# A hybrid encoder layer on one core: another order of work inside three of its four layer norms

## The chip, the cores and the metric

The kernel runs on one core of one Trainium2 chip. The metric is the device time of one execution in microseconds (us); of several executions the median is taken. A core has five engines that run at the same time and meet only through semaphores: PE (TensorE, matrix products; PEld are its weight loads), DVE (VectorE), ACT (ScalarE), POOL (GpSimd) and SP (SyncE, which here only starts transfers). An engine takes its own instructions strictly in the order in which they are written, so a waiting instruction holds up all that is written behind it.

## What is computed

512 tokens and 16 meta tokens of width 1024 go through one layer with three residual parts and four layer norms:

```python
h = layer_norm(concat([meta, x]), ln_in)                       # norm 0
h = layer_norm(A*h + 0.5*swiglu(h, gate1, up1, down1), ffn1)   # norm 1
h = layer_norm(A*h + token_mixer(h), mix)                      # norm 2
h = layer_norm(A*h + 0.5*swiglu(h, gate2, up2, down2), ffn2)   # norm 3
return h[:, N_META:]

def layer_norm(x, g, b):
    mu = mean(x)
    xc = x - mu
    return xc * rsqrt(mean(xc*xc) + eps) * g + b
```

The hidden width of a SwiGLU is 2816. The token mixer projects h, runs windowed attention and a gated linear attention in two directions, and projects back with w_out. A is the fourth root of 2. All of it is float32 in the reference.

## The kernel before

Everything is kept transposed: 128 of the 1024 features on the partitions, tokens along the free dimension, so h (`H`), the sum before a norm (`X`) and its scaled copies (`xs`) are 8 tiles of 128x528 (128x512 from norm 2 on, where the meta tokens are dropped). A product in float32 precision is made of three float16 products: weights and activations are each scaled by a power of two and split into a high part (f16) and a low part (the rest).

**Weights.** They come in 73 chunks into two slots of `stage`, in float32. For each chunk `c` DVE takes the largest magnitude of a partition (`chunk_max`, L1308, cmax), POOL takes it over all partitions (L1842, call), DVE makes the scale out of it in four small steps and the factor that undoes it in a fifth (`chunk_scale`: L1290 to L1295 and L1336), ACT writes the high part (`split_hi`, L951), and DVE the low part (`chunk_lo`, L1330), whose semaphore `w_ready` lets PE use the chunk and SP load the next chunk into its slot. The last tiles of each residual product are therefore followed by the weight work for the next stage: by norm 1 chunks IN0 and IN0+1 of w_in, by norm 2 chunks GU[1] and GU[1]+1 of the second SwiGLU.

**A layer norm** (norm L, tokens in two halves h = 0, 1). DVE adds each finished residual tile to a running sum; the last tile (7) is written in halves (`residual_tile`, L1359). PE gets the mean over the partitions by products with a constant matrix (L455, L465). DVE subtracts the mean in 8 steps for each half (`centre`, L1257). ACT squares these 8 tiles (L918), PE sums the squares (L470, 8 float32 products, recorded as 16), ACT takes the root of a half (L932, std), DVE its reciprocal (L1277, rstd). ACT's order is: squares of half 0, root of half 0, squares of half 1, root of half 1. Only when both reciprocals are there does DVE multiply tile by tile (L1281), ACT write `xs` (L943) and `H` (L945), and DVE the low part of `xs` (L1271); the first products of the next stage follow tile by tile. After four tiles ACT puts in the high part of the next weight chunk, for which it needs that chunk's scale.

**Tables.** ACT has one set of function tables loaded at a time. Before an activation whose function is not in it, the compiler puts an ACT_TABLE_LOAD. The root and the SiLU of the SwiGLU are in different sets.

The order of every engine's work is written out by hand; no scheduler is at work.

## Time and profile before

| | |
|---|---|
| median of 3 runs | 1099.26 us |
| the three runs | 1098.03, 1099.26, 1104.86 us |
| the profiled execution | 1098.44 us |
| its span, first to last instruction | 1096.6 us |
| mean granted clock of TensorE, of full speed | 0.972 |
| PE busy | 1005.5 us, 92% |
| DVE busy | 730.0 us, 67% |
| ACT busy | 385.6 us, 35% |
| table loads of ACT | 15, each 1283 ns |

The profiled execution lies 1.84 us above its own span (start and end of the program) and 0.82 us below the median of the three runs. PE is busy for nearly all of the span; the four layer norms are where it stands still, since nothing of the next stage can start before the norm is done.

### The profile page before, as it was taken

The numbers are of one execution on the slowest core, as the hardware profiler recorded it, in microseconds if no ns is written. First come the engines' busy times: TensorE is split into PE (matmuls) and PEld (weight loads), VectorE is DVE, ScalarE is ACT, GpSimd is POOL, SyncE is SP. The second block draws the span as 40 slices with busy tenths as digits, with TensorE's granted clock in tenths as the row PEclk, the third lists the DMA queues.
The fourth block names the chain that finished last, engine by engine and source line by source line (L and its number), as shares of the span: only waits on it lengthen the run. The fifth ranks groups of instructions, "written<-read, shape, count | busy, mean of one in ns | idle before, by whom it ended". The sixth has DMA issues, their size and how long they took to land.

```text
span 1096.6 us, 16402 instructions
## 1 busy us (share of the span) xinstructions
PE 1005.5 (92%) x6604; PEld 658.2 (60%) x6604; DVE 730.0 (67%) x1188; ACT 385.6 (35%) x492; POOL 33.8 (3%) x96
## 2 busy tenths in 40 slices
PE   2799999999899997999996889779999999989995
PEld 1588888888688874895565434434444444434443
DVE  7756666668865657777658857676666666876645
ACT  2722222224511117655234742362222222541105
POOL 1000000000000000000000000000000000000000
PEclk9899999999899998999998989889999999999998
DMA  4232232323313220221211002213232232312202
GB/s 157 71 114 101 90 111 80 115 77 140 109 54 106 96 77 1 78 78 40 76 40 39 1 1 77 77 39 113 79 115 103 88 115 90 145 56 103 105 1 78
DMA packets 25168, 88.70 MB, mean 81 GB/s; under 512 B 2859, under 2 KB 5123, under 8 KB 25123
## 3 DMA queue, kind: packets, MB, share of 16 engines
q1 hardware_dynamic: 24256, 87.24, 22.7%
q10 hardware_dynamic: 867, 0.85, 0.3%
q8 instruction: 29, 0.48, 0.2%
q14 instruction: 16, 0.13, 0.0%
HBM read 85.99 MB, written 2.10 MB: 80 GB/s over the span
## 4 chain that ended last, share of the span: by engine, by line
PE 75%; DVE 15%; ACT 7%; issue 2%; DMA 1%; ACTq 0%; POOL 0%; DVEq 0%
PE PS L485 35%; PE PS L521 20%; PE PS L576 8%; PE PS L872 3%; DVE cmax L1308 3%; DVE wsp L1330 3%; PE PS L470 2%; ACT wsp L951 2%; ACT H L945 2%; DVE X L1257 1%; PE PS L560 1%; PE PS L850 1%; DVE big L1408 1%; ACT xs L943 1%; PE PS L698 1%
## 5 line engine op out<-in xcount | busy, mean ns | idle before, releaser
L485 PE MATMUL PS<-xs,wsp 128*128 128x264 f16 (+1 forms) x3168 | 471.6, 312 | 12.8 <-ACT xs L943 8.1
L485 PEld LDWEIGHTS PS<-xs,wsp 128*128 128x128 f16 x3168 | 310.6, 98 | 173.8 <-issue 13.5
L951 ACT ACTIVATE wsp<-stage,wscale 128x2048 f16<-128x2048 f32 (+2 forms) x73 | 156.5, 2144 | 370.5 <-DVE wscale L1294 198.6
L1330 DVE SCALAR_TENSOR_TENSOR wsp<-stage,wscale,wsp 128x2048 f16<-128x2048 f32 (+2 forms) x73 | 184.6, 2529 | 113.9 <-ACT wsp L951 113.9
L521 PE MATMUL PS<-big,wsp 128*128 128x264 f16 (+1 forms) x1584 | 238.5, 314 | 11.6 <-DVE big L1408 9.5
L521 PEld LDWEIGHTS PS<-big,wsp 128*128 128x128 f16 x1584 | 155.8, 99 | 94.0 <-DVE big L1408 12.8
L1308 DVE TENSOR_REDUCE cmax<-stage 128x1 f32<-128x2048 f32 (+2 forms) x73 | 179.7, 2461 | 3.9
L1342 DVE SCALAR_TENSOR_TENSOR big<-PS,oscale,tmp_a 128x528 f32 (+3 forms) x44 | 33.4, 758 | 75.8 <-ACT tmp_a L958 75.8
L958 ACT ACTIVATE tmp_a<-PS,oscale 128x528 f32<-128x528 f32 (+1 forms) x44 | 30.5, 693 | 135.9 <-PE PS L485 135.9
L576 PE MATMUL PS<-xs,wsp 128*128 128x264 f16 (+1 forms) x384 | 67.0, 328 | 0.1
L1842 POOL PARTITION_ALL_REDUCE call<-cmax x73 | 29.5, 404 | 984.2 <-DVE cmax L1308 984.2
L470 PE MATMUL PS<-tmp_b,ones 128*128 128x264 f32 (+1 forms) x128 | 36.2, 445 | 17.5 <-ACT tmp_b L918 17.5
L576 PEld LDWEIGHTS PS<-xs,wsp 128*128 128x128 f16 x384 | 35.8, 98 | 24.4 <-issue 1.9
L872 PE MATMUL PS<-xs,wsp 128*128 128x512 f16 x192 | 42.4, 379 | 3.2 <-DVE X L1354 2.1
L470 PEld LDWEIGHTS PS<-tmp_b,ones 128*128 128x128 f32 x128 | 27.9, 223 | 26.1 <-ACT tmp_b L918 21.1
L918 ACT ACTIVATE tmp_b<-X 128x264 f32<-128x264 f32 (+1 forms) x64 | 23.9, 416 | 49.5 <-DVE X L1257 45.7
L576 PE MATMUL PS<-wsp,xs 128*88 128x256 f16 (+2 forms) x408 | 39.5, 257 | 1.7 <-ACT kT L1013 1.7
L981 ACT ACTIVATE big<-big,hscale 128x528 f16<-128x528 f32 (+1 forms) x44 | 30.3, 722 | 29.1 <-DVE big L1408 26.5
L576 PEld LDWEIGHTS PS<-wsp,xs 128*88 128x88 f16 (+2 forms) x408 | 38.0, 113 | 3.5 <-ACT kT L1013 2.5
L1408 DVE SCALAR_TENSOR_TENSOR big<-big,hscale 128x528 f16<-128x528 f32 (+1 forms) x44 | 31.6, 755 | 5.0 <-ACT big L981 3.8
L872 PEld LDWEIGHTS PS<-xs,wsp 128*128 128x128 f16 x192 | 18.5, 98 | 26.8 <-DVE wsp L1330 2.6
L1366 DVE SCALAR_TENSOR_TENSOR X<-PS,oscale,H 128x528 f32<-128x528 f32 (+1 forms) x16 | 12.2, 760 | 27.5 <-PE PS L521 27.4
(178 smaller groups left out, 694.4 us busy)
## 6 DMA issues: line engine op xcount, KB each, us to landing
stage<-in_gate SPq DMA_DIRECT2D x44, 512.0 KB, 3.7
stage<-in_up SPq DMA_DIRECT2D x44, 512.0 KB, 4.5
stage<-in_down SPq DMA_DIRECT2D x32, 704.0 KB, 4.9
stage<-in_w_in SPq DMA_DIRECT2D x16, 512.0 KB, 4.6
stage<-in_w_out SPq DMA_DIRECT2D x8, 512.0 KB, 4.3
X<-in_xT SPq DMA_DIRECT2D x2, 1056.0 KB, 6.9
out_T<-H SPq DMA_DIRECT2D x8, 256.0 KB, 2.0
stage<-in_w_in SPq DMA_DIRECT2D x2, 576.0 KB, 4.3
```

The lines of the kernel that those rows point to most:

```text
L470: nc.tensor.matmul(PS[:, ln_bank(L, 1, h), 0:ln_width(L)], ones[:, :], squares[:, n % 4, 0:ln_width(L)], start=k == 0, stop=k == KD - 1).t ...
L485: return nc.tensor.matmul(dst, w, x, start=k == 0 and wp + xp == 0, stop=k == KD - 1 and xp == 1)
L521: mm = nc.tensor.matmul(dst, w(wp, k), x, start=k in (0, split_at) and wp + xp == 0, stop=k + 1 in (kt, split_at) and xp == 1)
L576: mm = nc.tensor.matmul(dst, x if lhs_is_x else w, w if lhs_is_x else x, start=k == 0 and wp + xp == 0, stop=k == KD - 1 and xp == 1)
L872: mm = nc.tensor.matmul(acc(1, 2 * (n % 2)), w, tokens(1, xs[:, xp, k, :]), start=gla and k == REP and wp + xp == 0, stop=not gla and k == ...
L951: nc.scalar.activation(wsp[:, slot, 0, 0:cols], stage[:, slot, 0:cols], ACT.Copy, scale=wscale[:, slot:slot + 1]).then_inc(w_hi, 1)
L958: nc.scalar.activation(tokens(f, tmp_a[:, s, :]), acc(f, 4 * s), ACT.Silu, scale=oscale[:, slot:slot + 1]).then_inc(silu_ready, 1)
L981: nc.scalar.activation(hid_s[:, m, 0, ln_cols(2 * f)], hid[:, m + 2, ln_cols(2 * f)], ACT.Copy, scale=hscale[:, i:i + 1]).then_inc(hs_hi, 1)
L1308: nc.vector.tensor_reduce(cmax[:, one], stage[:, slot, 0:cols], AX.X, ALU.max, apply_absolute_value=True).then_inc(w_max, 1)
L1330: nc.vector.scalar_tensor_tensor(wsp[:, slot, 1, 0:cols], stage[:, slot, 0:cols], wscale[:, one], wsp[:, slot, 0, 0:cols], ALU.mult, ALU.s ...
L1342: nc.vector.scalar_tensor_tensor(tokens(f, hid[:, m + 2, :]), acc(f, 4 * s + 2), oscale[:, slot:slot + 1], tokens(f, tmp_a[:, s, :]), ALU. ...
L1408: nc.vector.scalar_tensor_tensor(hid_s[:, m, 1, t], hid[:, m + 2, t], hscale[:, i:i + 1], hid_s[:, m, 0, t], ALU.mult, ALU.subtract).then_ ...
```

## The change

Four edits:

- In norm 1 and norm 2 DVE's `chunk_max` of the second weight chunk moves from ahead of the centring to behind it.
- In the same norms `chunk_scale` of that chunk moves from ahead of the two reciprocals to behind them.
- In the last pass of the out projection, `chunk_lo` of chunk GU[1] moves from behind residual tile 7 to ahead of it.
- In every norm ACT gets one more instruction, a root of one column of a constant into an unused column of `warm`, ahead of the first square. It waits for nothing in norms 1 to 3.

```diff
@@ sb("warm") @@
-        warm = sb("warm", [P, 2])
+        warm = sb("warm", [P, 5])
@@ scalar: layer_norm(L) @@
                 if L == 0:
                     act.wait_ge(par_loaded, 16)
                     act.wait_ge(ready0, 6)
+                nc.scalar.activation(warm[:, L + 1:L + 2], eps[:, 1:2], ACT.Sqrt).then_inc(warmed, 1)
                 for h in range(2):
@@ vector: layer_norm(L, chunk) @@
                 if L:
                     for h in range(2):
                         centre(L, h)
-                if chunk is not None:
+                if L in (1, 2):
+                    c = (IN0, GU[1])[L - 1] + 1
+                    chunk_max(c, c % 2, c // 2, KD * 2 * P)
+                if chunk is not None and L == 0:
                     chunk_scale(*chunk)
...
                     nc.vector.reciprocal(rstd[:, half], std[:, half]).then_inc(rstd_ready, 1)
+                if chunk is not None and L:
+                    chunk_scale(*chunk)
                 dve.wait_ge(rstd_ready, 2 * L + 2)
@@ vector: main order @@
             ffn(0)
-            chunk_max(IN0 + 1, (IN0 + 1) % 2, (IN0 + 1) // 2, KD * 2 * P)
             layer_norm(1, (IN0 + 1, (IN0 + 1) % 2, XF_INQ))
...
                 for t in range(2):
+                    if last and t:
+                        chunk_lo(c + 1, (c + 1) % 2, cols)
                     residual_tile(2 * n + t, t, KD + 2 * n + t, c % 2, 2)
 
-            chunk_lo(GU[1], GU[1] % 2, GU_COLS)
-            chunk_max(GU[1] + 1, (GU[1] + 1) % 2, (GU[1] + 1) // 2, GU_COLS)
             layer_norm(2, (GU[1] + 1, (GU[1] + 1) % 2, XF_GU[1]))
```

How the rows of the engines move, with each kernel's own line numbers (a line of the changed kernel is up to 6 higher). First DVE from the last residual tile (X<-PS,oscale_b,X) to the multiplication (X<-X,stats) in norm 1; before, then with the change:

```order
L1359 SCALAR_TENSOR_TENSOR X<-PS,oscale_b,X 128x264 x2
L1308 TENSOR_REDUCE cmax<-stage 128x1
L1257 TENSOR_TENSOR X<-X,PS 128x264 x16
L1290 TENSOR_SCALAR cexp<-call 128x1
L1292 TENSOR_SCALAR cneg<-cexp 128x1
L1294 TENSOR_SCALAR wscale<-cneg 128x1
L1295 TENSOR_SCALAR winv<-cneg 128x1
L1336 TENSOR_TENSOR oscale<-winv,xinv 128x1
L1277 RECIPROCAL stats<-stats 128x264 x2
L1281 TENSOR_TENSOR X<-X,stats 128x528 x3
```
```order
L1365 SCALAR_TENSOR_TENSOR X<-PS,oscale_b,X 128x264 x2
L1258 TENSOR_TENSOR X<-X,PS 128x264 x16
L1314 TENSOR_REDUCE cmax<-stage 128x1
L1281 RECIPROCAL stats<-stats 128x264 x2
L1296 TENSOR_SCALAR cexp<-call 128x1
L1298 TENSOR_SCALAR cneg<-cexp 128x1
L1300 TENSOR_SCALAR wscale<-cneg 128x1
L1301 TENSOR_SCALAR winv<-cneg 128x1
L1342 TENSOR_TENSOR oscale<-winv,xinv 128x1
L1287 TENSOR_TENSOR X<-X,stats 128x528 x3
```

The maximum (cmax) has gone behind the 16 steps of centring (X<-X,PS), and the five small steps behind the two reciprocals, directly ahead of the multiplication.

DVE in the same place of norm 2, from the last running sum (stats<-stats,X) to the reciprocals; before, then with the change:

```order
L1250 TENSOR_TENSOR stats<-stats,X 128x512
L1359 SCALAR_TENSOR_TENSOR X<-PS,oscale,H 128x256 x2
L1330 SCALAR_TENSOR_TENSOR wsp<-stage,wscale,wsp 128x2048
L1308 TENSOR_REDUCE cmax<-stage 128x1
L1257 TENSOR_TENSOR X<-X,PS 128x256 x16
L1290 TENSOR_SCALAR cexp<-call 128x1
```
```order
L1251 TENSOR_TENSOR stats<-stats,X 128x512
L1336 SCALAR_TENSOR_TENSOR wsp<-stage,wscale,wsp 128x2048
L1365 SCALAR_TENSOR_TENSOR X<-PS,oscale,H 128x256 x2
L1258 TENSOR_TENSOR X<-X,PS 128x256 x16
L1314 TENSOR_REDUCE cmax<-stage 128x1
L1281 RECIPROCAL stats<-stats 128x256 x2
```

The low part (wsp<-stage,wscale,wsp) now stands ahead of the last residual tile (X<-PS,oscale,H in halves), the maximum behind the centring.

ACT from the last weight chunk of the first SwiGLU's stage to the second root of norm 1; before, then with the change:

```order
L951 ACTIVATE wsp<-stage,wscale 128x2304
L918 ACTIVATE tmp_b<-X 128x264 x8
L932 ACT_TABLE_LOAD
L932 ACTIVATE stats<-PS,eps 128x264
L918 ACTIVATE tmp_b<-X 128x264 x8
L932 ACTIVATE stats<-PS,eps 128x264
```
```order
L952 ACTIVATE wsp<-stage,wscale 128x2304
L925 ACT_TABLE_LOAD
L925 ACTIVATE warm<-eps 128x1
L918 ACTIVATE tmp_b<-X 128x264 x8
L933 ACTIVATE stats<-PS,eps 128x264
L918 ACTIVATE tmp_b<-X 128x264 x8
L933 ACTIVATE stats<-PS,eps 128x264
```

The table load has gone from between squares and root to ahead of the squares, together with the new one-column root. At the start of the kernel (norm 0) two loads stood before, one ahead of the squares and one ahead of the root:

```order
L918 ACT_TABLE_LOAD
L918 ACTIVATE tmp_b<-X 128x264 x8
L951 ACTIVATE wsp<-stage,wscale 128x2048
L932 ACT_TABLE_LOAD
L932 ACTIVATE stats<-PS,eps 128x264
```
```order
L925 ACT_TABLE_LOAD
L925 ACTIVATE warm<-eps 128x1
L918 ACTIVATE tmp_b<-X 128x264 x8
L952 ACTIVATE wsp<-stage,wscale 128x2048
L933 ACTIVATE stats<-PS,eps 128x264
```

Of these two one is left, ahead of the one-column root. In all, ACT_TABLE_LOAD stands 15 times before and 14 times with the change; nothing on PE, POOL or SP has moved.

## Rows read from the trace of the kernel before

**Rows 1.** The page: the chain of work that ended last, shares by engine.

```profile
...
PE 75%; DVE 15%; ACT 7%; issue 2%; DMA 1%; ACTq 0%; POOL 0%; DVEq 0%
...
```

**Rows 2.** Timeline, norm 1: start us, us, engine line op tiles xcount [idle<-releaser].

```profile
...
408.75 0.89 DVE L1359 SCALAR_TENSOR_TENSOR X<-PS,oscale_b,X 128x264 f32<-128x264 f32 x2 [2.12 <-PE PS L521]
...
409.56 2.28 DVE L1308 TENSOR_REDUCE cmax<-stage 128x1 f32<-128x2048 f32 x1
411.75 5.51 DVE L1257 TENSOR_TENSOR X<-X,PS 128x264 f32<-128x264 f32 x16
...
412.20 3.05 ACT L918 ACTIVATE tmp_b<-X 128x264 f32<-128x264 f32 x8 [11.77 <-DVE X L1257]
...
412.68 3.83 PE L470 MATMUL PS<-tmp_b,ones 128*128 128x264 f32 x16 [2.22 <-ACT tmp_b L918]
415.27 1.28 ACT L932 ACT_TABLE_LOAD   x1
416.56 0.48 ACT L932 ACTIVATE stats<-PS,eps 128x264 f32<-128x264 f32 x1
...
417.18 0.14 DVE L1290 TENSOR_SCALAR cexp<-call 128x1 int32<-128x1 int32 x1
...
417.88 1.80 DVE L1277 RECIPROCAL stats<-stats 128x264 f32<-128x264 f32 x1
...
421.79 1.80 DVE L1277 RECIPROCAL stats<-stats 128x264 f32<-128x264 f32 x1 [2.11 <-ACT stats L932]
423.62 1.95 DVE L1281 TENSOR_TENSOR X<-X,stats 128x528 f32<-128x528 f32 x3
...
```

**Rows 3.** Timeline of norm 2, with the residual tiles ahead of it.

```profile
...
690.45 2.00 ACT L951 ACTIVATE wsp<-stage,wscale 128x2048 f16<-128x2048 f32 x1 [8.53 <-DVE winv L1295]
...
696.65 0.88 DVE L1359 SCALAR_TENSOR_TENSOR X<-PS,oscale,H 128x256 f32<-128x256 f32 x2 [4.50 <-PE PS L872]
...
697.45 2.34 DVE L1330 SCALAR_TENSOR_TENSOR wsp<-stage,wscale,wsp 128x2048 f16<-128x2048 f32 x1
...
701.90 5.38 DVE L1257 TENSOR_TENSOR X<-X,PS 128x256 f32<-128x256 f32 x16
...
702.81 6.25 PE L470 MATMUL PS<-tmp_b,ones 128*128 128x256 f32 x16 [4.49 <-ACT tmp_b L918]
...
709.10 0.47 ACT L932 ACTIVATE stats<-PS,eps 128x256 f32<-128x256 f32 x1 [0.69 <-PE PS L470]
...
714.20 1.75 DVE L1277 RECIPROCAL stats<-stats 128x256 f32<-128x256 f32 x1 [2.84 <-ACT stats L932]
...
```

**Rows 4.** Timeline of norm 3, which has no weight work in it.

```profile
...
1074.75 0.88 DVE L1359 SCALAR_TENSOR_TENSOR X<-PS,oscale_b,X 128x256 f32<-128x256 f32 x2 [2.03 <-PE PS L521]
...
1076.02 5.39 DVE L1257 TENSOR_TENSOR X<-X,PS 128x256 f32<-128x256 f32 x16 [0.40 <-PE PS L465]
...
1076.95 3.72 PE L470 MATMUL PS<-tmp_b,ones 128*128 128x256 f32 x16 [0.53 <-ACT tmp_b L918]
...
1080.77 0.47 ACT L932 ACTIVATE stats<-PS,eps 128x256 f32<-128x256 f32 x1
...
```

**Rows 5.** Timeline of norm 0, ACT alone.

```profile
...
16.41 1.28 ACT L918 ACT_TABLE_LOAD   x1 [16.41 <-DVE X L1257]
...
24.06 2.00 ACT L951 ACTIVATE wsp<-stage,wscale 128x2048 f16<-128x2048 f32 x1 [1.49 <-DVE wscale L1294]
26.08 1.28 ACT L932 ACT_TABLE_LOAD   x1
27.38 0.48 ACT L932 ACTIVATE stats<-PS,eps 128x264 f32<-128x264 f32 x1
...
```

**Rows 6.** Windows: from:to us, busy PE, PEld, DVE, ACT, POOL; PEclk, DMA, GB/s.

```profile
...
425.30:431.00 5.70, 5.27 (x22) 2.62 (x23) 5.17 (x9) 5.70 (x8) 0.00 (x0) 0.50 0.00 0
...
698.40:702.80 4.40, 0.00 (x0) 0.00 (x0) 4.40 (x5) 0.46 (x2) 0.35 (x1) 0.81 0.36 120
702.80:709.00 6.20, 6.19 (x16) 4.78 (x16) 5.07 (x19) 3.90 (x8) 0.00 (x0) 0.58 0.23 89
...
```

## The prediction

> **What bounds the kernel now.** I read the page first. Its chain of waits gives three quarters of the span to PE [rows 1], and PE is busy for 92% of it: inside the SwiGLUs and projections the kernel runs at PE's pace, and work taken from DVE or ACT there buys nothing. The change touches only the layer norms, so I went to the timelines of the four norms and asked at each step which of two inputs came last. Since all that follows a norm starts from its output tiles, a norm that ends x us earlier moves the rest of the program by x, unless the clock of PE changes too; so I read the granted clock in windows last.
>
> In norm 1 [rows 2] the reader should see DVE finish the last residual tile, take the weight maximum for 2.28 us, and only then begin to centre, at 411.75. PE has had the means long before: norm 3 has no weight work, and there centring begins 1.27 us after the last residual tile has begun (1074.75 to 1076.02) [rows 4]. The squares follow the first centred tile, PE's sums the first square, and the root the last sum. From the first root to the end ACT and PE set the pace: the second half's squares stand behind the first root in ACT's order, and the second reciprocal waited 2.11 us for its root. Norm 2 [rows 3] has two pieces of weight work ahead of the centring, the low part (2.34 us) and the maximum.
>
> The table load in norm 1 looks as if it were on the path, since the root follows it at once. It isn't alone there: it ends at 416.55, and PE's sums end at 412.68 + 3.83 = 416.51 [rows 2]. Take away either one, and the other still holds the root.
>
> **The change, part by part.** All times are offsets within one profiled execution.
>
> *Norm 0: the table load.* Before, ACT writes a weight chunk's high part from 24.06 to 26.06, loads the table at 26.08 and takes the root at 27.38 [rows 5]. The root shows no idle time before it, so the sums of its half were there, and the high part waited for DVE's scale, which does not move; the load alone is on the path, and without it the root comes 27.38 - 26.08 = 1.30 us earlier. The other load, ahead of the first square at 16.41, also goes ahead of the wait for DVE, into time in which ACT has nothing to do. That makes the first squares 1.28 us earlier and gains nothing more, because ACT then waits for the scale. **1.30 us gained.**
> What the ScalarE page of the Trainium skill ("ScalarE: Activation LUTs", section "What ACT_TABLE_LOAD costs") says speaks for more: a switch costs the 1283 ns load and some 1380 ns of drain, 2.66 us in all. The trace shows no drain here, since the root starts 0.02 us after the load [rows 5]; by the page the gain of norm 0 would be 2.66 and the time 1088.6.
>
> *Norm 1: the maximum behind the centring.* Centring starts at 408.75 + 1.27 = 410.02 in place of 411.75: 1.73 us earlier. Squares and sums follow, PE's from 410.95 to 414.78; the table is already there, so the root comes with the same 0.05 us after the sums, at about 414.82, 1.74 us earlier than 416.56. The second reciprocal moves with it, from 421.79 to 420.05. Is DVE free by then? Centring until 415.53, maximum until about 417.7, first reciprocal until about 419.5: free 0.6 us before it is wanted. So the maximum, 2.28 us that lay on the path, now fits into a wait, with 0.6 us to spare. The load itself goes to where ACT stood still for 11.77 us ahead of the squares [rows 2]. That covers its 1.28 us and the new root of one column, which costs between nothing and the 0.48 us of a root of 264 columns; without that cover both would delay the first square.
>
> *Norm 1: the scale behind the reciprocals.* Here is a cost. The five small steps took 0.70 us, from 417.18 to 417.88 [rows 2], while DVE had nothing urgent to do. Now they stand between the second reciprocal and the first multiplication, where nothing covers them. DVE starts an instruction that waits for nothing about 0.1 us before the last one is over (the maximum starts at 409.56, before 409.64), and the multiplication started 0.03 us after the reciprocal; so of the 0.70 I take 0.60 as added. The bounds are 0.5 (a second overlap) and 0.8 (none, and a wait). The weight maximum is over 4 us old by then, so POOL is no issue; ACT needs the scale only after four tiles. **1.74 - 0.60 = 1.14 us gained.**
>
> *Norm 2: two pieces out of the way.* The low part moves ahead of residual tile 7. It needs ACT's high part, done at 692.45, and DVE stood still for 4.50 us before 696.65, since 692.15 [rows 3]: it runs from about 692.5 to 694.8, 1.8 us before PE delivers tile 7, so the residual tile is not delayed. SP may then load the next chunk 5 us earlier, into a slot that nobody reads any more. Centring starts at 696.65 + 1.27 = 697.92 in place of 701.90: 3.98 us earlier.
>
> *Norm 2: the clock.* PE's sums for the first half took 6.25 us here [rows 3], against 3.72 in norm 3 [rows 4]. The windows say why: after 4.4 us without a product the granted clock began to fall (0.81), and during the sums it was 0.58 of full speed, so 1.2 GHz for most of it [rows 6]. With the change PE stands still for about 0.5 us between means and sums, as in norm 3, where the sums ran at 2.4 GHz. I take 3.72. The sums then run from 698.83 to 702.55 and the root comes at 702.59 instead of 709.10: 6.51 us earlier, 3.98 of it from order and 2.53 from the clock. DVE has the same 0.6 us to spare as in norm 1. Less 0.60 for the scale steps: **5.91 us gained**, the largest term.
>
> *Norm 3.* No weight work, one table load, ending at the same time as the sums (1076.95 + 3.72 = 1080.67, root at 1080.77) [rows 4]: **0.06 us gained.**
>
> **The sum:** 1.30 + 1.14 + 5.91 + 0.06 = 8.41 us. The profiled execution took 1098.44 us: 1090.0. It lies 0.82 under the median of the three runs, so a median of the new kernel may come out some tenths higher.
>
> **Rivals.**
>
> *The clock stays low in norm 2's first sums.* Then they take 6.25 us as now, and the gain falls by 2.53: **1092.6**. For it: the clock is already falling in some norms when the sums come. Against it: norm 1 had a stop of 2.22 us before its sums, longer than the 0.5 us expected here, and still needed only 3.83 us for them [rows 2]. Chance 0.10.
>
> *DVE becomes the bound inside the norm.* If maximum and first reciprocal used up more than the 0.6 us to spare, for instance because the maximum's chunk or DVE's own start comes later by a microsecond, each of the two norms would lose some 0.2 to 1 us, say 1.5 in all: **1091.5**. For it speaks only that the margin is small. Chance 0.06.
>
> *The clock is dealt better.* After norm 1 the first projection products ran at half clock (0.50 from 425.3 to 431) and were PE's to finish [rows 6]; half a stretch of 5.7 us less is 1.4 us of products less, if PE bounds them throughout: **1088.6**. Chance 0.12.
>
> *A table switch costs more than its load.* In norm 0 there is room for little: from the end of the high part to the root it is 1.32 us [rows 5], and the root may overlap the high part by 0.1, which makes 1.42 in place of 1.30: **1089.9**. Chance 0.02. This is what the rows leave of the drain in the page on ScalarE of the Trainium skill.
>
> *Slower than before.* One mechanism could do it: PE's stop between the sums and the next stage grows by the 0.60 us of the scale steps in norms 1 and 2, the clock falls sooner, and the low stretch after it lasts longer, in products that PE bounds. At half clock each us of such a stretch costs 0.5 us. The 8.41 us are used up once low clock in such products has grown by 16.8 us; the one after norm 1 holds at least 5.7 us now [rows 6]. So it would have to more than triple in norm 1, or be dealt anew all over the kernel, where the mean clock of 0.972 means 31 us at 2.4 GHz lost so far, of which a quarter more would have to come. **1099 to 1101**. The shown runs of the same program (1098.03, 1098.44 profiled, 1099.26) speak against so large a redeal, one at 1104.86 leaves room. "TensorE: Matmul & The Clock Gate" of the Trainium skill (section "What's actually happening") goes further than these runs: one kernel meets a different number of slow products from run to run, which would argue for a larger chance; the runs shown don't bear it out beyond 1.2 us, the last one apart. Chance 0.03; a milder form, 3 to 6 us lost (**1093 to 1096**), gets 0.06.
>
> *The change doesn't do what it says* would mean that a second load appears ahead of the squares, because square and root are in different sets. The instruction order rules it out: one load in each norm, none between squares and root.
>
> **How the numbers follow.** My forecast, all terms as summed, has 0.61 and by itself spans 1089 to 1091. Faster than that are the better clock and, barely, the dearer switch (0.14), slower the rest (0.25). For 8 in 10 the range goes down to 1087.6, which takes in the better clock and bounds of the small terms, and up to 1094.0, past the low clock in norm 2 and the DVE rival; the rest of the slower cases is outside. A measurement of this kernel tells a difference of about 1%, 11 us, from none. The forecast is 0.8%, so within: 0.90. Faster by over 1% would be under 1088.3, which needs the better clock in both places: 0.08. Slower by over 1%: 0.02.
>
> **What the new profile would show.** Norm 0: no load between high part and root, root near 26.1. Norm 1: centring 1.3 us after the last residual tile, maximum behind it, root right at the end of the sums, and the five small steps with about 0.6 us between second reciprocal and multiplication. Norm 2: low part ended before tile 7's residual starts, sums in 3.7 us at full clock. From the start of the last residual tile to the first multiplication it should take 13.7 us in norm 1 in place of 14.87 (408.75 to 423.62), and to the second reciprocal 11.0 us in norm 2 in place of 17.55 (696.65 to 714.20). Wrong would be: sums of 6 us in norm 2, a reciprocal that starts late behind the maximum, or norms that are shorter as said while the end does not move, which would put the loss into PE's clock in the stages between.

## The result and the profile after

The changed kernel took 1095.09 us, the median of 20 runs (1089.35 to 1096.02); the kernel before took 1098.52 in the same sessions, the median of 20 (1095.64 to 1104.86). The ratio is 0.9948, with a 95% interval of 0.9931 to 0.9965: a gain of 0.5%. That is 5.7 us by the means (1093.5 against 1099.2) and 3.4 us by the medians, where 8.4 were forecast. The median lies 1.1 us above the stated range; carried over by the ratio to the 1099.26 us known at the time of the forecast, the time is 1093.5 us, 0.5 inside it.

The single times say more than the median. They fall into two groups with nothing between: 7 of 20 at 1089.35 to 1090.80, with a mean granted clock of 0.969 to 0.973, and 13 of 20 at 1094.83 to 1096.02, with 0.966 to 0.968. The forecast of 1090.0 is the time of the lower group (mean 1090.0). The profiled execution is of the upper one: 1095.9 us, span 1094.1, clock 0.966, against 1098.44, 1096.6 and 0.972 before.

Inside the norms the profile after shows what was forecast. The timeline of norm 1, columns as in [rows 2]:

```profile
...
407.35 0.89 DVE L1365 SCALAR_TENSOR_TENSOR X<-PS,oscale_b,X 128x264 f32<-128x264 f32 x2 [2.12 <-PE PS L521]
...
408.64 5.53 DVE L1258 TENSOR_TENSOR X<-X,PS 128x264 f32<-128x264 f32 x16 [0.41 <-PE PS L465]
...
409.58 3.83 PE L470 MATMUL PS<-tmp_b,ones 128*128 128x264 f32 x16 [0.53 <-ACT tmp_b L918]
413.45 0.48 ACT L933 ACTIVATE stats<-PS,eps 128x264 f32<-128x264 f32 x1 [1.29 <-PE PS L470]
...
414.08 2.28 DVE L1314 TENSOR_REDUCE cmax<-stage 128x1 f32<-128x2048 f32 x1
...
416.27 1.80 DVE L1281 RECIPROCAL stats<-stats 128x264 f32<-128x264 f32 x1
...
418.67 1.80 DVE L1281 RECIPROCAL stats<-stats 128x264 f32<-128x264 f32 x1 [0.60 <-ACT stats L933]
420.39 0.10 DVE L1296 TENSOR_SCALAR cexp<-call 128x1 int32<-128x1 int32 x1
...
421.05 1.95 DVE L1287 TENSOR_TENSOR X<-X,stats 128x528 f32<-128x528 f32 x3
...
```

Centring begins 1.29 us after the last residual tile (408.64 - 407.35), where [rows 2] had 3.00; PE's stop before the sums is 0.53 in place of 2.22; the root comes right behind the sums, the maximum runs behind the centring and the first reciprocal behind it. The second reciprocal waited 0.60 us, so DVE had the margin that was forecast. Between its start and the multiplication lie 2.38 us, against 1.83 before: 0.55 for the five scale steps. From residual tile to multiplication: 13.70 us, 14.87 before.

The timeline of norm 2, which answers to [rows 3]:

```profile
...
695.36 2.35 DVE L1336 SCALAR_TENSOR_TENSOR wsp<-stage,wscale,wsp 128x2048 f16<-128x2048 f32 x1 [0.32 <-ACT wsp L952]
...
699.54 0.88 DVE L1365 SCALAR_TENSOR_TENSOR X<-PS,oscale,H 128x256 f32<-128x256 f32 x2 [1.82 <-PE PS L872]
...
700.81 5.39 DVE L1258 TENSOR_TENSOR X<-X,PS 128x256 f32<-128x256 f32 x16 [0.40 <-PE PS L465]
...
701.74 3.72 PE L470 MATMUL PS<-tmp_b,ones 128*128 128x256 f32 x16 [0.53 <-ACT tmp_b L918]
705.50 0.47 ACT L933 ACTIVATE stats<-PS,eps 128x256 f32<-128x256 f32 x1 [1.25 <-PE PS L470]
...
710.59 1.75 DVE L1281 RECIPROCAL stats<-stats 128x256 f32<-128x256 f32 x1 [0.53 <-ACT stats L933]
...
712.92 1.90 DVE L1287 TENSOR_TENSOR X<-X,stats 128x512 f32<-128x512 f32 x3
...
```

The low part ended at 697.71, 1.83 us before the residual tile. The sums took 3.72 us in place of 6.25 and the second reciprocal began 11.05 us after the residual tile. To the multiplication: 13.38 us, 19.33 before.

The timelines of norm 3 and, below it, of ACT alone in norm 0 answer to [rows 4] and [rows 5]:

```profile
...
1072.34 0.88 DVE L1365 SCALAR_TENSOR_TENSOR X<-PS,oscale_b,X 128x256 f32<-128x256 f32 x2 [2.03 <-PE PS L521]
...
1078.30 0.47 ACT L933 ACTIVATE stats<-PS,eps 128x256 f32<-128x256 f32 x1 [1.25 <-PE PS L470]
...
```

ACT in norm 0:

```profile
...
23.94 2.00 ACT L952 ACTIVATE wsp<-stage,wscale 128x2048 f16<-128x2048 f32 x1 [2.84 <-DVE wscale L1300]
25.84 0.46 ACT L933 ACTIVATE stats<-PS,eps 128x264 f32<-128x264 f32 x1
...
```

No load stands between high part and root in norm 0; the root came at 25.84 (26.08 was forecast), the first multiplication at 34.57 in place of 36.12. Of these 1.55 us 0.12 are no work of the change: DVE's first instruction, which waits for the input, began at 6.34 in place of 6.46. The other 1.43 are the load and an overlap: the root now starts 0.10 us before the high part is over, where it started 1.32 us after that. In norm 3 the multiplication came 12.84 us after the residual tile, 12.91 before.

By these marks the norms gave back 1.55 + 1.17 + 5.95 + 0.07 = 8.74 us. The span got shorter by 2.5. To find the rest I cut the program at its norms: from the first multiplication of one norm to the last residual tile of the next, and from there to the first multiplication again. In us, from the unrounded trace, so that the last digit can differ by one from a difference of the rows shown:

| kernel (profiled execution) | norm 0 to 1 | norm 1 | mixer, 1 to 2 | norm 2 | norm 2 to 3 | norm 3 | clock |
|---|---|---|---|---|---|---|---|
| before | 372.62 | 14.87 | 273.03 | 19.33 | 358.76 | 12.91 | 0.972 |
| after | 372.77 | 13.70 | 278.49 | 13.38 | 359.42 | 12.84 | 0.966 |

The mixer stretch, which the change doesn't touch, is 5.46 us longer, and between norm 2 and 3 another 0.66. The windows of the attention, at the end of the mixer, show where; columns as in [rows 6]. Those of before:

```profile
...
620.00:624.00 4.00, 3.87 (x24) 1.78 (x24) 3.27 (x15) 2.38 (x6) 0.00 (x0) 1.00 0.00 0
...
636.00:640.00 4.00, 4.00 (x14) 1.44 (x10) 2.63 (x13) 2.55 (x8) 0.00 (x0) 0.54 0.00 0
640.00:644.00 4.00, 4.00 (x16) 1.71 (x16) 1.60 (x8) 2.12 (x7) 0.00 (x0) 0.50 0.00 0
644.00:648.00 4.00, 4.00 (x19) 2.10 (x16) 1.50 (x5) 1.97 (x5) 0.00 (x0) 0.68 0.02 4
648.00:652.00 4.00, 2.94 (x13) 0.81 (x12) 2.16 (x3) 1.96 (x4) 0.00 (x0) 1.00 0.00 0
...
```

And of after:

```profile
...
616.00:620.00 4.00, 1.85 (x8) 1.57 (x8) 3.08 (x12) 2.60 (x8) 0.00 (x0) 0.75 0.02 4
620.00:624.00 4.00, 4.00 (x15) 1.29 (x15) 2.38 (x10) 2.46 (x7) 0.00 (x0) 0.50 0.00 0
624.00:628.00 4.00, 4.00 (x17) 2.06 (x16) 0.83 (x3) 1.13 (x4) 0.00 (x0) 0.50 0.00 0
628.00:632.00 4.00, 4.00 (x26) 1.91 (x26) 2.15 (x10) 2.21 (x6) 0.00 (x0) 0.97 0.00 0
...
636.00:640.00 4.00, 3.28 (x18) 1.42 (x18) 3.35 (x20) 2.32 (x8) 0.00 (x0) 0.81 0.00 0
640.00:644.00 4.00, 4.00 (x16) 1.85 (x16) 1.90 (x7) 2.46 (x7) 0.00 (x0) 0.50 0.00 0
644.00:648.00 4.00, 4.00 (x14) 1.29 (x14) 1.33 (x7) 1.96 (x6) 0.00 (x0) 0.50 0.00 0
...
```

In these stretches the granted clock is low once before, from 636 to some point past 644. After, it is low twice: from about 618 to 628 as well, with PE busy throughout. What PE did just ahead of the first of these is the same in both. PE's timeline at the transposes of attention unit 8 and, last row, of unit 12, before:

```profile
...
620.13 1.06 PE L832 MATMUL PS<-ident,tmp_a 128*128 128x128 f32 x8 [2.21 <-DVE tmp_a L1732]
...
622.20 2.08 PE L850 MATMUL PS<-big,arena 16*64 16x512 f32 x8
...
634.01 0.85 PE L832 MATMUL PS<-ident,tmp_a 128*128 128x128 f32 x6 [1.98 <-DVE tmp_a L1732]
...
```

The same instructions after:

```profile
...
618.15 1.94 PE L832 MATMUL PS<-ident,tmp_a 128*128 128x128 f32 x8 [2.21 <-DVE tmp_a L1738]
...
622.04 3.87 PE L850 MATMUL PS<-big,arena 16*64 16x512 f32 x8
...
636.72 0.85 PE L832 MATMUL PS<-ident,tmp_a 128*128 128x128 f32 x6 [1.99 <-DVE tmp_a L1738]
...
```

PE stands still for 2.21 us ahead of unit 8 in both, waiting for DVE's tile. Before, the clock stays at 2.4 GHz and the two groups shown take 1.06 and 2.08 us; after, it falls to 1.2 GHz and they take 1.94 and 3.87. The second stop, 1.98 and 1.99 us ahead of unit 12, was followed by the low clock in both.

### The profile page after: what moved, and what is told of

Read it like the earlier page. It is cut to its first block, busy times and chain, and to the rows that moved or that the text cites. A ratio compares the mean times of both kernels' runs of the same rounds, so it can differ in the third digit from the quotient of the medians.

```text
span 1094.1 us, 16405 instructions
## 1 busy us (share of the span) xinstructions
PE 1009.9 (92%) x6604; PEld 658.6 (60%) x6604; DVE 729.9 (67%) x1188; ACT 385.2 (35%) x495; POOL 33.8 (3%) x96
## 4 chain that ended last, share of the span: by engine, by line
PE 75%; DVE 15%; ACT 7%; issue 2%; DMA 1%; ACTq 0%; POOL 0%; DVEq 0%
PE PS L485 35%; PE PS L521 20%; PE PS L576 8%; PE PS L872 3%; DVE wsp L1336 3%; DVE cmax L1314 3%; ACT wsp L952 2%; DVE X L1258 2%; PE PS L470 2%; ACT H L946 2%; PE PS L850 1%; PE PS L560 1%; DVE big L1414 1%; ACT xs L944 1%; PE PS L698 1%
## 5 line engine op out<-in xcount | busy, mean ns | idle before, releaser
L470 PE MATMUL PS<-tmp_b,ones 128*128 128x264 f32 (+1 forms) x128 | 33.8, 422 | 10.2 <-ACT tmp_b L918 10.2
```

The costliest lines, as they stand in the source:

```text
L470: nc.tensor.matmul(PS[:, ln_bank(L, 1, h), 0:ln_width(L)], ones[:, :], squares[:, n % 4, 0:ln_width(L)], start=k == 0, stop=k == KD - 1).t ...
```

## The experiments

Each kernel ran beside the kernel before on the same chip; a median is given with its ratio to that and the 95% interval. Theory A is that the norms gave all that was forecast, and that PE's two stops of 2 us in the attention, after which the clock falls in some executions, took it back.

**again**: the changed kernel as it is.

> The changed kernel once more, unaltered. Theory A (the 5.5 us that were lost between norm 1 and norm 2 are a stretch of half clock of TensorE in the attention, which comes in some executions and not in others): single times fall into two groups, near 1090 and near 1095, none between; the mean granted clock of the first is higher (0.97) than that of the second (0.966). If the profile is of the first group, the attention has one low stretch less and the distance from norm 1's first multiplication to norm 2's last residual tile is 273 us, as before; if of the second, 278.5 us. Theory B (the new order costs the mixer something fixed, whatever the clock): all executions lie near 1095 and the distance is 278.5 us every time.

1090.74 us (9 runs, 1089.39 to 1096.00), 0.9937 (0.9917 to 0.9958). Again two groups: 7 runs up to 1091.12, 2 at 1094.76 and 1096.00. The profiled execution was of the upper group (1096.0) and had a mixer of 278.48 us and both low stretches, the one of *after* to 0.01 us.

**fill_att**: the changed kernel, with products of no use put into both stops, after the last product that can be issued and before the wait for DVE. Their results are read by nobody.

```diff
+            def filler(bank, n):
+                for _ in range(n):
+                    nc.tensor.matmul(PS[:, bank, 0:P], ones[:, :], ones[:, :], start=True, stop=True)
...
+                if u in (8, 12):
+                    pe.wait_ge(s_max, 2 * (u + 1))
+                    filler(2 * (u % 2), 8)
                 att_transposes(u)
```

> The changed kernel, with 8 products of a constant (1.9 us at full clock) for PE, result unused, ahead of the transposes of attention units 8 and 12, where it stands still for 2.2 and 2.0 us. Theory A: with PE busy there neither low stretch begins in the attention after the first units; both cost about 5 us, so the distance from norm 1's first multiplication to norm 2's last residual tile falls from 278.5 to about 268 us and the time to about 1085, in one group. Theory B: the products fit into the stops and change nothing: 1095, distance 278.5 us.

1086.48 us (6 runs, 1085.77 to 1089.21), 0.9900 (0.9873 to 0.9927), 1.5 above what was expected. PE's timeline at unit 8:

```profile
...
615.46 2.05 PE L879 MATMUL PS<-ones 128*128 128x128 f32 x16
617.74 1.06 PE L832 MATMUL PS<-ident,tmp_a 128*128 128x128 f32 x8 [0.23 <-DVE tmp_a L1745]
...
```

Its windows:

```profile
...
616.00:620.00 4.00, 3.77 (x32) 2.90 (x32) 3.08 (x12) 2.60 (x8) 0.00 (x0) 1.00 0.00 0
...
636.00:640.00 4.00, 3.67 (x24) 1.65 (x22) 2.52 (x11) 2.65 (x8) 0.00 (x0) 1.00 0.00 0
640.00:644.00 4.00, 2.15 (x13) 1.39 (x14) 2.83 (x8) 3.88 (x8) 0.00 (x0) 1.00 0.00 0
...
```

The fillers take 2.05 us, the stop shrinks to 0.23, the transposes start no later, and the clock stays at 2.4 GHz. The mixer took 269.81 us: 8.68 less than *after* (268 was expected). None of the six times is in the upper group. This is the main evidence for Theory A: nothing was taken out of the program, something was added, and its median is 4.3 us under that of *again* and 8.6 under that of *after*.

**before_fill**: the same edit in the kernel before.

> The kernel before, with the same 16 products of a constant at the same two places. Theory A: its profile had one low stretch there (636 to 646 us), so it should lose that: distance 268 us instead of 273, time near 1093.5; and the spread between its executions should shrink. Theory B: no change, 1098.5.

1095.76 us (12 runs, 1094.43 to 1098.05), 0.9981 (0.9966 to 0.9996). The mixer took 269.43 us, 3.60 less than before, so that one low stretch in the attention costs 3.6. The median is 2.3 above what was expected (1093.5); the spread shrank as expected, and none of the 12 times is near 1104.5. But norm 1 took 16.56 us in place of 14.87: PE's stop of 2.2 us between means and sums, which the change removes, was here followed by the low clock (0.50 from 414 to 416), while in *before* it was not. The old order has an uncertain stop inside norm 1 too. The profiled execution of *lo_only* below, which has norm 1 in the old order, shows it a second time: 16.54 us.

**fill_8**: the changed kernel, fillers ahead of unit 8 alone (`if u in (8,)`).

> The changed kernel with PE's stop ahead of attention unit 8 filled (8 products of a constant), that ahead of unit 12 left. Theory A (a stop of some 2 us lets the clock fall in some executions and not in others, and each is dealt by itself): the low stretch after unit 8 never comes, so the group near 1095 disappears and all times lie near 1089 to 1091; the distance from norm 1's first multiplication to norm 2's last residual tile is 273 us if the stretch after unit 12 comes, 270 if not. The rival (the stops only matter together, or the slow group has another cause): the group near 1095 stays.

1090.00 us (6 runs, 1088.02 to 1093.71), 0.9923 (0.9904 to 0.9941). Four of the six lie where all were expected, 1088.02 and 1093.71 don't; the group near 1095 is not among them. Mixer 272.89 us, one low stretch as before the change. Its windows:

```profile
...
620.00:624.00 4.00, 4.00 (x26) 1.78 (x24) 3.14 (x14) 3.23 (x8) 0.00 (x0) 1.00 0.00 0
...
636.00:640.00 4.00, 4.00 (x18) 2.37 (x18) 1.73 (x7) 1.39 (x3) 0.00 (x0) 0.50 0.00 0
...
```

So in the profiled executions of the changed kernel with and without these fillers two low stretches go with about 1096, one with 1091, none with 1086.4. I infer that the lower group of the changed kernel has one of the two; no execution of it was profiled. If so, the forecast of 1090.0 met that group because the profiled execution it started from had one such stretch as well, which the forecast hadn't looked at.

**lo_only**: the kernel before, with the low part alone moved ahead of tile 7.

```diff
+                    if last and t:
+                        chunk_lo(c + 1, (c + 1) % 2, cols)
...
-            chunk_lo(GU[1], GU[1] % 2, GU_COLS)
```

> The kernel before with one of the four edits: the low part of chunk GU[1] ahead of residual tile 7. PE then waits about 2.2 us instead of 4.49 us between the means and the sums of norm 2. If the clock holds over 2.2 us, as it did in norm 1, the sums take 3.72 us and norm 2 ends 2.26 + 2.53 = 4.8 us earlier (second reciprocal 12.8 us after the last residual tile begins, before 17.55); if it does not, only 2.3 us earlier (15.3 us). The total time also carries the clock of the attention, by up to 5 us.

1095.26 us (13 runs, 1092.40 to 1103.02), 0.9976 (0.9960 to 0.9993). The profiled execution is the slowest, with both low stretches in the attention (278.50 us). Norm 2 in it:

```profile
...
703.44 0.88 DVE L1359 SCALAR_TENSOR_TENSOR X<-PS,oscale,H 128x256 f32<-128x256 f32 x2 [1.83 <-PE PS L872]
...
706.43 5.37 DVE L1257 TENSOR_TENSOR X<-X,PS 128x256 f32<-128x256 f32 x16
...
707.34 5.36 PE L470 MATMUL PS<-tmp_b,ones 128*128 128x256 f32 x16 [2.23 <-ACT tmp_b L918]
...
713.31 1.75 DVE L1277 RECIPROCAL stats<-stats 128x256 f32<-128x256 f32 x1 [0.81 <-ACT stats L932]
...
```

Norm 2 took 16.25 us, 3.08 less than before. The maximum is still ahead of the centring, PE's stop is 2.23 us, and the sums of the first half took 5.36 us in place of 3.72, with the clock low for a part of them. That is between the two cases expected. So in this execution the low part alone didn't buy the fast clock; in *after* the maximum's move made the stop 0.53, and the sums ran at full clock. That is one execution with a stop of a length that has shown both outcomes; the maximum's move alone wasn't tried.

**no_table**: the changed kernel without the early root, so that each load stands where it stood before.

```diff
-                nc.scalar.activation(warm[:, L + 1:L + 2], eps[:, 1:2], ACT.Sqrt).then_inc(warmed, 1)
```

> The changed kernel without its new one-column roots, so that the table loads stand where they stood before. By the working of the prediction: in norm 0 the root comes 1.3 us later (27.3 instead of 25.84), since nothing hides the load there; in norms 1, 2 and 3 the load of 1283 ns ends together with PE's sums and costs under 0.1 us each (norm 1 from the last residual tile to the first multiplication 13.7 us as with the change, norm 2 13.4, norm 3 12.9). The rival (the loads were on the path in every norm, 1.3 us each): 15.0, 14.7 and 14.1 us, some 5 us in all. The total is noisy by 5 us from the attention's clock; with 1.4 us more in all the groups of single times should lie near 1091 and 1092 (and 1096), not near 1089.4 and 1090.7.

1092.50 us (12 runs, 1090.91 to 1098.38), 0.9947 (0.9925 to 0.9969), again in two groups: 7 up to 1092.54, 5 from 1096.52. The norms 1, 2 and 3 took 13.72, 13.45 and 12.90 us: a load that ends with the sums costs at most 0.07. In norm 0 it costs its full length:

```profile
...
24.11 2.00 ACT L951 ACTIVATE wsp<-stage,wscale 128x2048 f16<-128x2048 f32 x1 [1.47 <-DVE wscale L1299]
26.13 1.28 ACT L932 ACT_TABLE_LOAD   x1
27.42 0.48 ACT L932 ACTIVATE stats<-PS,eps 128x264 f32<-128x264 f32 x1
...
```

The root comes 1.31 us after the high part's end, in *after* 0.10 before it: 1.41 in all, and the first multiplication moves by 1.42 once the start of the input is taken off. The lower group of times begins 1.5 us higher (1090.91 against 1089.39). "ScalarE: Activation LUTs" of the Trainium skill ("What ACT_TABLE_LOAD costs") adds a drain of some 1380 ns to the load. The trace doesn't agree: the root follows the load by 0.01 us. The measurement decides: an exposed load costs 1.3 us, and 0.1 more for the overlap of two activations that it prevents.

**scale_mid**: the changed kernel, the five scale steps between the two reciprocals, where DVE waits.

```diff
                     nc.vector.reciprocal(rstd[:, half], std[:, half]).then_inc(rstd_ready, 1)
-                if chunk is not None and L:
-                    chunk_scale(*chunk)
+                    if chunk is not None and L and h == 0:
+                        chunk_scale(*chunk)
```

> The changed kernel with the five small scale steps of norms 1 and 2 between the two reciprocals, where DVE stands still for 0.60 and 0.53 us, instead of behind both. If the steps cost what stands in the trace (second reciprocal to multiplication 2.38 us instead of 1.84), 13.70 becomes 13.2 in norm 1 and 13.38 becomes 12.9 in norm 2, about 1.0 us in all. If instead the steps are then late for the second reciprocal (POOL's maximum over the partitions, or the 0.70 us of the steps against 0.6 of stop), no more than 0.3 us is gained.

1092.32 us (6 runs, 1088.57 to 1094.38), 0.9934 (0.9913 to 0.9955). Norm 1 and 2 took 13.16 and 12.87 us, 0.54 and 0.51 less. Norm 1:

```profile
...
418.01 0.09 DVE L1296 TENSOR_SCALAR cexp<-call 128x1 int32<-128x1 int32 x1
...
418.69 1.80 DVE L1281 RECIPROCAL stats<-stats 128x264 f32<-128x264 f32 x1
420.53 1.95 DVE L1287 TENSOR_TENSOR X<-X,stats 128x528 f32<-128x528 f32 x3
...
```

The reciprocal starts when it did, and the multiplication 1.84 us after it. The median of the whole doesn't show it: the times spread over 6 us, and in the profiled execution both low stretches came in the attention, though the first was shorter than in *after*, and the mixer took 275.84 us.

**fill_all**: scale_mid, with fillers also at unit 0, after norms 1 and 2 and ahead of the first down-projection tiles.

```diff
             layer_norm(1)
+            filler(6, 15)
...
+                if k == 15:
+                    filler(2, 17)
...
+                if u == 0:
+                    pe.wait_ge(o_done, PAIRS * NCH)
+                    filler(4, 16)
```

> The changed kernel with the scale steps between the reciprocals and with products of a constant in every long stop of PE at full clock: 15 ahead of the first products after norms 1 and 2 (stops of 4.6 us), 17 in the first down tile of each SwiGLU (4.7 us), 16 ahead of attention unit 0 (4.4 us), 8 ahead of units 8 and 12. If half clock after a stop is what costs, each of the low stretches that follow goes: 3.4 us at each down tile (6.8 us at half clock, PE bound), about 1 us after norm 1, little after norm 2 and in the first attention units, where ACT and DVE bound it; with 1.0 us from the scale steps, 1086.5 - 6.8 - 1 - 1.0 = about 1077.5. Against: where the products run into the end of a stop they delay real work by up to 1 us each; then 1080. If the clock falls regardless: 1086.

1084.47 us (5 runs, 1080.66 to 1086.66), 0.9865 (0.9844 to 0.9885): a miss of 7. The distances tell why. Norm 2 to 3 took 358.74 us, the same as with low stretches in *fill_att*, and norm 0 to 1 0.75 less than there: the low clock at those places costs little, which I read as PE not being what others wait for there (argued from the distances, not tried by itself; the length counts too: with low clock of 3.4 us at the down-projection tiles norm 0 to 1 took 371.69 in *fill_8*, with 6.8 us 372.43 in *fill_att*). And in the profiled execution the clock fell behind two stops that had been left and had not been followed by low clock in *fill_att*: 2.15 us ahead of output tile 2 and, ahead of unit 15:

```profile
...
639.65 0.85 PE L837 MATMUL PS<-ident,tmp_b 128*128 128x128 f32 x6 [2.19 <-DVE tmp_b L1751]
...
```

The window behind it:

```profile
...
640.00:644.00 4.00, 4.00 (x15) 1.73 (x14) 1.84 (x3) 1.67 (x4) 0.00 (x0) 0.58 0.01 4
...
```

**quiet_before, quiet_after, quiet_mid**: the kernel before, the changed kernel and scale_mid, with fillers in every stop of 2 us or more outside norm 0: those of fill_all, unit 15 and output tile 2, and in quiet_before also between means and sums of norms 1 and 2 (the second edit below, in that kernel alone). This compares the orders with the clock nearly the same (0.993, 0.992 and 0.990).

```diff
+                if n == 2:
+                    filler(1, 8)
                 out_part(n, True)
...
+                if L in (1, 2):
+                    filler(6, (8, 16)[L - 1])
```

> The kernel before with PE kept busy by products of a constant in all its stops of 2 us and more: between means and sums of norm 1 (8) and norm 2 (16), after norms 1 and 2 (15 each), in the first down tiles (17), and ahead of attention units 0, 8, 12, 15 and of out tile 2. The clock should then stay full after the start. If the change's worth were the order alone, this kernel and the next one (the same with the change) tell it without the clock: by the terms of the prediction 1.30 (table) + 1.14 (norm 1) + 5.91 - 2.53 (norm 2 without its clock term) + 0.06 = 5.9 us. I expect 1087 here, with a spread between executions of 1 to 2 us instead of 9. Rival: the reordering is worth as much as the profiled executions differ by median, 3.4 to 7 us, whatever the clock, or less than 3 us.

> The changed kernel with the same products of a constant, but for the two places between means and sums, where it has no long stop. Theory: full clock throughout, 1081, 5.9 us under quiet_before, spread 1 to 2 us; fill_all, which left the stops ahead of unit 15 and out tile 2, had half clock after both in its profile and a median of 1084.5 with 1080.7 as its best. If those two stops are not what is left, the median stays near 1084.

> quiet_after with the scale steps of norms 1 and 2 between the two reciprocals: 13.17 and 12.87 us from the last residual tile to the first multiplication as in fill_all, so 1.0 us less than quiet_after: 1080. This is the version meant to beat both kernels.

quiet_before: 1090.13 us (7 runs, 1089.35 to 1091.17), 0.9924 (0.9895 to 0.9953). quiet_after: 1083.27 (6 runs, 1082.90 to 1084.47), 0.9862 (0.9830 to 0.9894). quiet_mid: 1082.68 (6 runs, 1080.78 to 1083.28), 0.9852 (0.9819 to 0.9884), the lowest median of all; it beats both kernels, 1.5% under before, but it and quiet_after can't be told apart by the whole time (the intervals overlap), only by the norms (0.54 and 0.51 us). All three came out 2.3 to 3.1 us above what was expected (1087, 1081, 1080). The granted clock in 40 slices, of quiet_after:

```profile
...
PEclk9899999999999999999999999999999999999998
...
```

The spread, 6.7 us for the changed kernel, is 1.6 in quiet_after. The change is then worth 6.86 us by the medians, and no time of one kernel reaches the other's. The two profiled executions differ by 7.86 us. By distances: norm 0 with its load 1.51 (0.09 of it the input), norm 1 1.17, norm 2 3.48, norm 3 0.06, mixer 1.60. The forecast without its term for the clock is 8.41 - 2.53 = 5.88, and the distances without the mixer give 6.2.

The 1.60 of the mixer are not the change's. They are one more low stretch in quiet_before, and it is not behind a stop of 2 us. Twelve products of the mixer in quiet_before, which had no stop longer than 0.62 us for 20 us before them:

```profile
...
519.83 4.45 PE L583 MATMUL PS<-xs,wsp 128*128 128x512 f16 x12
...
```

The same twelve in quiet_after, with the same stops before them:

```profile
...
517.24 2.76 PE L581 MATMUL PS<-xs,wsp 128*128 128x512 f16 x12
...
```

So filling the long stops made low clock rarer, but didn't rule it out.

| kernel (profiled execution) | norm 0 to 1 | norm 1 | mixer, 1 to 2 | norm 2 | norm 2 to 3 | norm 3 | clock |
|---|---|---|---|---|---|---|---|
| fill_att | 372.43 | 13.70 | 269.81 | 13.38 | 358.74 | 12.84 | 0.980 |
| before_fill | 371.69 | 16.56 | 269.43 | 19.46 | 358.75 | 12.90 | 0.975 |
| fill_8 | 371.69 | 13.70 | 272.89 | 13.38 | 359.59 | 12.84 | 0.971 |
| scale_mid | 372.70 | 13.16 | 275.84 | 12.87 | 359.53 | 12.84 | 0.971 |
| fill_all | 371.68 | 13.17 | 270.50 | 12.87 | 358.74 | 12.84 | 0.987 |
| quiet_before | 371.69 | 14.87 | 269.11 | 16.86 | 358.74 | 12.90 | 0.993 |
| quiet_after | 371.68 | 13.70 | 267.51 | 13.38 | 358.74 | 12.84 | 0.992 |
| quiet_mid | 371.69 | 13.16 | 267.43 | 12.87 | 358.74 | 12.84 | 0.990 |

## Why the prediction was right inside the norms and wrong in the sum

- *Norm 0, 1.30.* Measured 1.43, without the 0.12 us of the earlier input; without the early load 1.42 of it is lost again. Right, and the 0.1 over it is the overlap of root and high part that the forecast had named with the dearer switch (1.42).
- *Norm 1, 1.74 - 0.60 = 1.14.* Measured 1.17. The scale steps cost 0.55, and the 0.6 us margin of DVE was 0.60.
- *Norm 2, 3.98 + 2.53 - 0.60 = 5.91.* Measured 5.95. The sums took 3.72 us, the stop ahead of them 0.53. With the clock held up in both kernels it is 3.48, against 3.98 - 0.60 = 3.38. One argument against low clock there was weaker than it looked: the 2.22 us stop of norm 1 with fast sums behind it was one execution, and in *before_fill* and *lo_only* the same stop was followed by low clock.
- *Norm 3, 0.06.* Measured 0.07.
- *The table load in norm 1 is not alone on the path.* Shown by no_table.
- *The rivals inside the norm* (slow sums, DVE as the bound) did not occur. Of the dearer switch the 0.1 us of overlap came, and nothing more.

**The step that failed** is the one that the sum stands on: "a norm that ends x us earlier moves the rest of the program by x, unless the clock of PE changes too". I then treated the exception as a rival of 0.06 (1093 to 1096, the milder form of the slower case), and it came in half of the executions: 15 of the 29 of the unchanged new kernel lie in the upper group (13 of 20 in the first sessions, 2 of 9 in *again*). I gave it too little because I had priced the redeal by the one stretch after norm 1 [rows 6], and hadn't looked for PE's stops in the stages that the change leaves alone. That the norms are where PE stands still, as "Time and profile before" says, is not so: outside them *before* has stops of 4.73 and 4.77 us at the first down-projection tiles, 4.39 at attention unit 0 and three of about 2 us. Its trace showed 2.21 us ahead of unit 8 with the clock unharmed and 1.98 ahead of unit 12 with the clock low. Two stops of nearly one length with two outcomes say that the length doesn't settle it, the two groups of times of one kernel say that the program doesn't either, and at 3.1 to 5.5 us each, in products that PE bounds, they are as large as the terms of the sum. The runs shown, which agree within 1.2 us but for one, looked like evidence against it; three of them can't show a second group. What did come is what the prediction gave as its last sign of being wrong: norms shorter as said, while the end does not move as much, with the loss in PE's clock in the stages between.

That the loss lies behind these stops is shown three ways: the distances put into the mixer 5.46 of the 6.3 us that the norms gave back and the span lacks; with fillers in the two stops it is out (269.81), and none of six times is in the upper group; and with all long stops filled the two orders differ by 6.86 us. "TensorE: Matmul & The Clock Gate" of the Trainium skill ("What's actually happening") says, of the products at a kernel's start, that one kernel meets a different number of slow ones from run to run. The runs agree, and not for the start alone, with two groups of times and granted clocks for one kernel; the traces show eight transposes at 1.06 or 1.94 us behind the same stop, in two kernels. The page adds that the penalty is under 1% of a typical span. For one stretch that holds here (5.5 of 1095), but so small was the whole change, and what all long stops together cost is at the page's bound (0.9948 of before against 0.9862 with them filled).

**What stays open:** why the changed kernel falls into its upper group in half of its executions, when the kernel before has so high a time (1104.47 and more) in 10 of 75, and what else spreads the other times of before over 1095.2 to 1100.4. The five profiled executions with a low stretch behind unit 8 are of *after*, *again*, *no_table*, *scale_mid* and *lo_only*, kernels with the new and the old order alike, so the order of the norms doesn't decide it alone; whether it is only where the stop falls in time wasn't tried.

## What to carry to other kernels

Before forecasting a gain under 1%, list PE's stops of two microseconds in the whole program, not only where the edit is, and price each as "may cost half a stretch of products or nothing". If their sum is as large as the gain, forecast two groups of times, and give the second a real chance. Such a stop is cheap to close with a few products of no use ahead of the wait; over all long stops it made either order 0.6 to 1.1% faster by the medians, at least as much as the change itself is worth, and the times steadier. It doesn't make the clock certain: *quiet_before* had a low stretch without such a stop. And where five small steps must run between two waits, put them into the wait: 0.5 us each time.

## What the runs showed of the hardware

- Stops of 1.98 to 2.23 us were followed by the low clock in some profiled executions and not in others, for the same instructions. Those of 4.0 to 4.8 us, at unit 0, after norms 1 and 2 and at the first down-projection tiles, had low clock during or right behind them in all nine profiled executions that left them open.
- Shorter stops are no safeguard. In quiet_before the clock was low from 520.2 to 523.6 with no stop over 0.62 us in the 20 us before it, and in quiet_after from 423.0 to 426.4, behind fillers and stops of 1.30 and 0.82 us.
- One low stretch behind a 2 us stop cost 3.1 to 3.6 us of the mixer (272.89 against 269.81, 273.03 against 269.43) and the second one, in *after*, 5.5 (278.49 against 273.03).
- With eight products of 128x128 ahead of the wait (2.05 us, a stop of 0.23 left) the clock stayed at 2.4 GHz behind the stop in every profiled execution that had them at unit 8 (seven) or unit 12 (six).
- In the SwiGLUs low clock cost little that can be seen, which I read as PE waiting for others there, not tried by itself: between norm 2 and 3 *before* and *fill_att* took 358.76 and 358.74 us with low stretches at the first down-projection tile (a window of 4 us at 0.65 and 0.66), *fill_all* and *quiet_after* 358.74 without, and *after*, with a longer one (0.50 in one window, 0.81 in the next), 359.42.
